# Two transformer blocks on one core: both heads' stick-breaking values in turn, and a projection that begins with three tiles side by side

## The chip, the cores and the metric

The kernel runs on one core of one Trainium2 chip. The metric is the device time of one execution in microseconds; of the runs shown the median is taken. The weights come from memory during the run; nothing of them stays from one execution to the next.

## The reference

Two blocks work on 512 tokens of width 1024. The first has three mixers, whose outputs are gated, added, projected and normed, and a feed-forward part; the second has a gated recurrence, latent attention and two convolutional feed-forward parts. The change touches only the first block's stick-breaking attention (8 heads of 64) and the projection behind the merge:

```python
def stick_breaking_attention(q, k, v):
    # A[t,s] = sigmoid(z_ts) * prod_{s<j<t} (1 - sigmoid(z_tj)), s < t
    def one_block(args):
        q_blk, bi = args
        z = jnp.einsum('bhqd,bhkd->bhqk', q_blk, kf) * scale
        mask = key_pos < qpos
        log1m = jnp.where(mask, jax.nn.log_sigmoid(-z), 0.0)
        excl = lax.cumsum(log1m, axis=3, reverse=True) - log1m
        a = jnp.where(mask, jnp.exp(jax.nn.log_sigmoid(z) + excl), 0.0)
        return jnp.einsum('bhqk,bhkd->bhqd', a, vf)
...
merged = gates[:, :, 0] * y_pool + gates[:, :, 1] * y_sb + gates[:, :, 2] * y_x
h = h + rmsnorm(merged @ w_out[l], norm_mix_post[l])
```

## The kernel before, in words

Activations lie transposed: a tile has 128 features on the partitions and the 512 tokens beside each other; eight tiles are one activation. Every product with a weight is done three times, for precision: high half of the weight by high half of the operand (L225), low by high (L226), high by low (L227). An output tile of 128 features is `pe_tile`: 8 blocks of contraction, 24 products, into one bank of `ps_gemm` (four banks, `m.gb`) or `ps_attend` (four banks, `m.ab`). A unit is the weight of one such tile, 512 KB. There are four slots for units: SyncE loads unit u when GpSimd is done with unit u-4, ScalarE writes its high half (`high`, L200) when TensorE is done with unit u-4, and GpSimd the low half (L2454 and L2455). TensorE waits in `take_unit` for both halves.

The order on each engine is written out by hand, with semaphore waits between them; there is no scheduler. Each of the four stick-breaking rounds (`pe_stick`) does two heads: tiles for query, key and value, the scores of head 0 (L740, and the mask, L743), the values' transposes (L349), two gate tiles, the suffix sums of head 0 (`pe_stick_suffix`, L755), a gate tile, the scores of head 1, head 0's values (`pe_stick_values`, L766), a gate tile, the pooled products, and the suffix sums of head 1. Head 1's values stand behind the query tile of the next round, behind the fourth round behind the first gate tile of the merge. ScalarE makes softplus and its high half from the scores (L827 to L836), VectorE the rest (L906, L909), which is the suffix sums' operand, and ScalarE's exponential (L842) makes the weights that the values multiply. `act_stick_out` (L847) and `dve_stick_low_out` (L892) take both heads' result.

The values are plain fp32 products; in the trace each product has two records and two weight loads. The output has 64 rows: head 0 writes partitions 0 to 63 of bank `ab(3)`, head 1 partitions 64 to 127. The cross attention before it has such products too, L596, in this order (r is the first output partition, 0 for even h and 64 for odd; all 512 tokens wide):

```python
    for j in range(2):
        for h in (2 * j, 2 * j + 1):
            k, r = (h % 2) * 2 + h // 2, 64 * (h % 2)
            for mb in range(2):
                ins = t.op.matmul(m.a_bank[r:r + 64, j * 512:(j + 1) * 512],
```

`pe_merge` does the second gate and the attention's output projection, two tiles at a time; VectorE gates (L996), adds (L1000) and, behind ScalarE's high half (L980), writes the low half of each merged tile (L1002). `pe_project_mix` multiplies the merged tiles by w_out, in eight tiles; ScalarE copies each result out (L1025) and squares it (L281), VectorE adds the squares (L301), and TensorE sums them over the partitions (L257) for the norm. `pe_wide` is the other way to do tiles: three at a time, block of contraction by block, so that it can begin when the first operand is there; the norms' first tiles use it.

Of the kernel before, what the change touches and what calls it, by code (L numbers as in the profile page):

```python
# [7 lines left out]
P = 128  # L8
S = 512
D = 1024  # L10
KD = D // P
# [6 lines left out]
TB = S // P  # L18
TILE = S
# [3 lines left out]
SLOTS = 4  # L23
WIDE = 3
# [5 lines left out]
ZOFF = (0, 512, 1024, 896)  # L30
# [8 lines left out]
ACT = mybir.ActivationFunctionType  # L39
# [67 lines left out]
class Memory:  # L107
# [50 lines left out]
    def bank(self, b, w=512):  # L158
        return self.gb(b, w) if b < 4 else self.ab(b - 4, w)
# [23 lines left out]
def short_unit(m, u):  # L183
    return unit_source(m, u)[0]


def high(m, s):

    if s.ahead:
        s.ahead = False  # L190
        return
    u = s.unit
    s.unit += 1
    if u >= m.n_units:
        return
    j, w = u % SLOTS, UNIT_S if short_unit(m, u) else UNIT
    s.wait_ge(m.s_raw[j], 16 * (u // SLOTS + 1))
    if u >= SLOTS:
        s.wait_ge(m.U.sem, u - SLOTS + 1)
    s.op.activation(m.wh[:, j * UNIT:j * UNIT + w], m.raw[:, j * UNIT:j * UNIT + w], ACT.Copy).then_inc(m.s_hi, 1)  # L200


def unit_of(m, *event):

    return m.U.table[event] - 1


def high_to(m, s, u):

    while s.unit <= min(u, m.n_units - 1):  # L210
        high(m, s)


def take_unit(m, t, ahead=0):

    u = t.unit + ahead
    t.wait_ge(m.s_hi, u + 1)
    t.wait_ge(m.s_lo, u + 1)
    return (u % SLOTS) * UNIT


def products(m, t, out, base, pairs, start=True, stop=True):
    for n, (blk, xh, xl) in enumerate(pairs):
        c = base + blk * P
        t.op.matmul(out, m.wh[:, c:c + P], xh, start=start and n == 0, stop=False, skip_group_check=True)  # L225
        t.op.matmul(out, m.wl[:, c:c + P], xh, start=False, stop=False, skip_group_check=True)  # L226
        ins = t.op.matmul(out, m.wh[:, c:c + P], xl, start=False, stop=stop and n == len(pairs) - 1,  # L227
                          skip_group_check=True)
    return ins


def pe_tile(m, t, event, out, xh, xl, quarters=range(4)):

    base = take_unit(m, t)
    w = TILE
    for q in quarters:
        pairs = [(kb, xh[:, kb * w:(kb + 1) * w], xl[:, kb * w:(kb + 1) * w]) for kb in (2 * q, 2 * q + 1)]
        ins = products(m, t, out, base, pairs, start=q == 0, stop=q == 3)
        if q == 3:
            ins.then_inc(*m.U.mark(*event))  # L240
            t.unit += 1


def pe_wide(m, t, kb, events, xh, xl):

    sl = slice(kb * TILE, (kb + 1) * TILE)
    bases = [take_unit(m, t, n) for n in range(WIDE)]
    for b, base in enumerate(bases):
        ins = products(m, t, m.gb(b), base, [(kb, xh[:, sl], xl[:, sl])], start=kb == 0, stop=kb == KD - 1)
        if kb == KD - 1:  # L250
            ins.then_inc(*m.U.mark(*events[b]))
    if kb == KD - 1:
        t.unit += WIDE


def pe_sum_over_partitions(m, t, event, out, src):
    t.op.matmul(out, m.col("ones", 0, P), src, start=True, stop=True).then_inc(*m.T.mark(*event))  # L257
# [17 lines left out]
def act_square(m, s, stage, j, src, width=TILE):  # L275
    if j == 0:
        s.op.activation(m.ss[:, 0:width], src, ACT.Square).then_inc(*m.A.mark(stage, "square", j))
        return
    if j > 2:
        s.wait_ge(*m.V.at(stage, "sum", j - 2))  # L280
    s.op.activation(m.sq_tile(j % 2, width), src, ACT.Square).then_inc(*m.A.mark(stage, "square", j))  # L281
# [65 lines left out]
def pe_to_tokens(m, t, event, bank, src, blocks):  # L347
    for b in range(blocks):
        ins = t.op.transpose(bank[:, b * P:(b + 1) * P], src[:, b * P:(b + 1) * P], m.col("ident", 0, P))  # L349
    ins.then_inc(*m.T.mark(*event))  # L350
# [353 lines left out]
def stick_tiles(m):  # L704
    c = KD + 4
    lg = [m.big[:, c * TILE + n * ZW:c * TILE + (n + 1) * ZW] for n in range(2)]
    return m.big_tile(KD), m.big_tile(KD + 1), m.big_tile(KD + 2), m.big_tile(KD + 3), lg
# [49 lines left out]
    ins.then_inc(*m.T.mark("stick", "suffix", i, hh))  # L757


def pe_stick_values(m, t, i, hh):  # L760
    _, _, _, vtok, lg = stick_tiles(m)
    r, x = 64 * hh, lg[hh]
    t.wait_ge(*m.A.at("stick", "vtok", i))
    t.wait_ge(*m.A.at("stick", "weights", i, hh))
    for kb in range(TB):
        ins = t.op.matmul(m.a_bank[r:r + 64, 3 * 512 + kb * P:4 * 512], vtok[:, kb * P + r:kb * P + r + 64],  # L766
                          x[:, ZOFF[kb]:ZOFF[kb] + S - kb * P], start=kb == 0, stop=kb == 3, skip_group_check=True)
    ins.then_inc(*m.T.mark("stick", "out", i, hh))


def pe_stick_pooled(m, t, i):
# [14 lines left out]
def stick_bank(m, n, i):  # L786

    return m.gb(n if i else (2, 3, 0)[n])


def pe_stick(m, t, i):
    vt = stick_tiles(m)[2]
    for n, name in enumerate(("q", "k", "v")):
        if i:
            t.wait_ge(*(m.V.at("stick", "pooled", i - 1, 0) if n == 2 else m.V.at("stick", f"gate{2 * n}", i - 1, 1)))
        elif n == 2:
            t.wait_ge(*m.A.at("cross", "kept", 6))
        else:
            continue
        pe_tile(m, t, ("stick", name, i), stick_bank(m, n, i), m.nh, m.nl)  # L800
        if i and n == 0:
            pe_stick_values(m, t, i - 1, 1)
    pe_stick_scores(m, t, i, 0)
    t.wait_ge(*m.V.at("stick", "v", i))
    t.wait_ge(*(m.V.at("stick", "low", i - 1) if i else m.A.at("cross", "kept", 7)))
    pe_to_tokens(m, t, ("stick", "vtok", i), m.ab(3), vt, TB)
    t.wait_ge(*m.V.at("stick", "q", i))
    pe_tile(m, t, ("stick", "gate0", i, 0), m.gb(0), m.nh, m.nl)
    pe_tile(m, t, ("stick", "gate2", i, 0), m.gb(1), m.nh, m.nl)
    pe_stick_suffix(m, t, i, 0)  # L810
    t.wait_ge(*m.V.at("stick", "gate0", i, 0))
    pe_tile(m, t, ("stick", "gate0", i, 1), m.gb(0), m.nh, m.nl)
    pe_stick_scores(m, t, i, 1)
    pe_stick_values(m, t, i, 0)
    t.wait_ge(*m.V.at("stick", "gate2", i, 0))
    pe_tile(m, t, ("stick", "gate2", i, 1), m.gb(1), m.nh, m.nl)
    pe_stick_pooled(m, t, i)
    pe_stick_suffix(m, t, i, 1)
# [132 lines left out]
def pe_merge(m, t):  # L951
    for j in range(0, KD, 2):
        for n in range(2):
            t.wait_ge(*(m.V.at("merge", "gate", j - 2 + n) if j else m.V.at("stick", "gate0" if n == 0 else "gate2", 3, 1)))
            pe_tile(m, t, ("merge", "gate", j + n), m.gb(n), m.nh, m.nl)
            if j == 0 and n == 0:
                pe_stick_values(m, t, 3, 1)
        base = take_unit(m, t)
        t.wait_ge(*m.V.at("stick", "low", 3))
        for n in range(2):  # L960
            t.wait_ge(*(m.V.at("merge", "gated", j - 2 + n) if j else m.V.at("stick", "pooled", 3, n)))
            pairs = [(4 * n + kb, m.bigr[:, O_HIGH + kb * TILE:O_HIGH + (kb + 1) * TILE],
                      m.bigr[:, O_LOW + kb * TILE:O_LOW + (kb + 1) * TILE]) for kb in range(4)]
            products(m, t, m.gb(2 + n), base, pairs).then_inc(*(m.U if n else m.T).mark("merge", "out", j + n))
        t.unit += 1
# [37 lines left out]
                .then_inc(*m.V.mark("merge", "low", j + n))  # L1003


def pe_project_mix(m, t):
    t.wait_ge(*m.V.at("merge", "low", 7))
    for j in range(KD):
        if j < 4:
            t.wait_ge(*(m.V.at("merge", "gate", 6 + j) if j < 2 else m.V.at("merge", "gated", 4 + j)))  # L1010
        else:
            t.wait_ge(*m.A.at("mixed", "kept", j - 4))
        pe_tile(m, t, ("mixed", j), m.gb(j % 4), m.bigr[:, 0:8 * TILE], m.bigr[:, 8 * TILE:16 * TILE])
    t.wait_ge(*m.V.at("mixed", "sum", KD - 1))
    pe_sum_over_partitions(m, t, ("mixed", "total"), m.ab(3), m.ss[:, :])


def act_project_mix(m, s):
    for j in range(KD):
        f = m.big_tile(j)  # L1020
        high(m, s)
        if j == 0:
            s.wait_ge(*m.V.at("merge", "low", 7))
        s.wait_ge(*m.U.at("mixed", j))
        s.op.activation(f, m.gb(j % 4), ACT.Copy).then_inc(*m.A.mark("mixed", "kept", j))  # L1025
        s.wait_ge(*m.A.at("mixed", "kept", j))
        act_square(m, s, "mixed", j, f)
    high_to(m, s, unit_of(m, "ffn0", "up", 0, 0, 0) + WIDE)
    s.tables(LOGEXP)
    s.wait_ge(*m.T.at("mixed", "total"))  # L1030
    act_rstd(m, s, ("mixed", "rstd"), m.rstd2, m.ab(3), D)
# [1643 lines left out]
```

## Time and profile before

| | us |
|---|---|
| median of 3 runs | 2090.29 (2089.08 to 2091.22) |
| the profiled execution itself | 2093.21 |
| its span, first to last instruction | 2091.4 |
| TensorE busy (matmul) | 2038.1 (97%) |
| VectorE, ScalarE, GpSimd busy | 916.7, 909.6, 847.8 |

The span is 1.8 us shorter than the execution that it is part of. PE is TensorE's matmul, PEld its weight load, DVE VectorE, ACT ScalarE, POOL GpSimd. A matmul of 512 columns is shown with some 0.39 us, but the next one starts 0.227 us after it, since they are pipelined: durations of single records overlap, and starts tell the rate. The granted clock is the share of TensorE's full clock of 2.4 GHz that it was given; over the whole span it is 0.992.

### The profile page before, as it was taken

How to read it: one execution, taken by the hardware profiler on the slowest of the kernel's cores; microseconds unless marked ns; L12 is line 12 of the kernel's file. 1: busy time of each engine (PE TensorE's matmuls, PEld its weight loads, DVE VectorE, ACT ScalarE, POOL GpSimd, SP SyncE). 2: the span in 40 equal slices, each digit the busy share in tenths (PEclk: the TensorE clock that was granted, in tenths of full speed). 3: DMA queues.
4: the chain of work that ended last, by engine and by line, in shares of the span. 5: the costliest groups of instructions: out<-in, count | busy, mean ns of one | idle time of the engine just before them, and what ended most of it. 6: DMA issues, size and time to landing. Idle time of an engine off the chain costs nothing.

```text
span 2091.4 us, 23319 instructions
## 1 busy us (share of the span) xinstructions
PE 2038.1 (97%) x9356; PEld 1659.9 (79%) x9356; DVE 916.7 (44%) x1436; ACT 909.6 (43%) x1254; POOL 847.8 (41%) x672
## 2 busy tenths in 40 slices
PE   7999999989999998999999999999999999999999
PEld 6777787768888886788887888888877778888887
DVE  5622223334310323877886355055154544531551
ACT  6455444244323323555555444234256644432441
POOL 1243333435444454233334354444432234444542
PEclk9999999999999999999999999999999999999999
DMA  6122222223333332112121233333310222332332
GB/s 240 51 80 71 81 68 74 81 81 91 101 100 88 104 94 88 41 61 71 52 70 61 81 111 101 101 91 101 100 44 26 84 71 81 111 99 83 106 96 71
DMA packets 51659, 178.09 MB, mean 85 GB/s; under 512 B 5728, under 2 KB 8928, under 8 KB 51424
## 3 DMA queue, kind: packets, MB, share of 16 engines
q1 hardware_dynamic: 51552, 176.61, 27.2%
q8 instruction: 74, 1.21, 0.2%
q14 instruction: 33, 0.27, 0.0%
HBM read 174.49 MB, written 2.10 MB: 84 GB/s over the span
## 4 chain that ended last, share of the span: by engine, by line
PE 93%; DVE 4%; ACT 2%; POOL 1%; issue 1%; DMA 0%; SPq 0%; ACTq 0%
PE ps_gemm L225 24%; PE ps_gemm L227 24%; PE ps_gemm L226 24%; PE ps_attend L225 3%; PE ps_attend L227 3%; PE ps_attend L226 3%; PE ps_attend L1415 2%; PE ps_attend L755 1%; PE ps_attend L2195 1%; PE ps_attend L740 1%; PE ps_attend L766 1%; PE ps_attend L2261 1%; PE ps_attend L2196 1%; PE ps_attend L257 1%; ACT weights_high L200 1%
## 5 line engine op out<-in xcount | busy, mean ns | idle before, releaser
L2454 POOL TENSOR_TENSOR weights_low<-weights_raw,weights_high 128x512 fp32r<-128x512 f32 (+1 forms) x334 | 423.4, 1268 | 1222.1 <-ACT weights_high L200 1221.7
L225 PE MATMUL ps_gemm<-normed_high,weights_high 128*128 128x512 f32 x1672 | 667.4, 399 | 14.5 <-DVE normed_low L286 12.3
L227 PE MATMUL ps_gemm<-normed_low,weights_high 128*128 128x512 f32 x1672 | 653.5, 391 | 0.0
L226 PE MATMUL ps_gemm<-normed_high,weights_low 128*128 128x512 f32 x1672 | 653.3, 391 | 0.0
L200 ACT ACTIVATE weights_high<-weights_raw 128x1024 fp32r<-128x1024 f32 (+1 forms) x341 | 340.7, 1005 | 440.2 <-PE ps_attend L227 208.4
L2455 POOL TENSOR_TENSOR weights_low<-weights_raw,weights_high 128x512 fp32r<-128x512 f32 (+1 forms) x334 | 440.0, 1317 | 0.0
L225 PEld LDWEIGHTS ps_gemm<-normed_high,weights_high 128*128 128x128 f32 x1672 | 315.7, 189 | 86.1 <-DVE normed_low L286 13.9
L226 PEld LDWEIGHTS ps_gemm<-normed_high,weights_low 128*128 128x128 f32 x1672 | 315.8, 189 | 66.6 <-issue 3.8
L227 PEld LDWEIGHTS ps_gemm<-normed_low,weights_high 128*128 128x128 f32 x1672 | 315.2, 188 | 66.8
L225 PE MATMUL ps_gemm<-operands_high_low,weights_high 128*128 128x512 f32 x576 | 227.6, 395 | 6.1 <-DVE operands_high_low L1002 3.3
L227 PE MATMUL ps_gemm<-operands_high_low,weights_high 128*128 128x512 f32 x576 | 225.4, 391 | 0.0
L226 PE MATMUL ps_gemm<-operands_high_low,weights_low 128*128 128x512 f32 x576 | 225.2, 391 | 0.0
L342 DVE TENSOR_TENSOR scratch<-ps_gemm,rstd 128x512 f32<-128x512 f32 x91 | 62.1, 688 | 249.1 <-PE ps_gemm L227 234.2
L342 DVE TENSOR_TENSOR squares<-ps_gemm,rstd 128x512 f32<-128x512 f32 x106 | 73.1, 690 | 173.4 <-PE ps_gemm L227 141.6
L1181 ACT ACTIVATE ps_attend<-squares,parameters 128x512 f32<-128x512 f32 x88 | 68.9, 783 | 170.1 <-DVE squares L342 170.1
L225 PEld LDWEIGHTS ps_gemm<-operands_high_low,weights_high 128*128 128x128 f32 x576 | 108.9, 189 | 30.3 <-DVE operands_high_low L1002 3.7
L225 PE MATMUL ps_attend<-operands_high_low,weights_high 128*128 128x512 f32 (+1 forms) x304 | 117.0, 385 | 10.6 <-DVE operands_high_low L286 10.6
L227 PEld LDWEIGHTS ps_gemm<-operands_high_low,weights_high 128*128 128x128 f32 x576 | 108.7, 189 | 23.1
L226 PEld LDWEIGHTS ps_gemm<-operands_high_low,weights_low 128*128 128x128 f32 x576 | 108.9, 189 | 22.4 <-issue 0.2
L226 PE MATMUL ps_attend<-operands_high_low,weights_low 128*128 128x512 f32 (+1 forms) x304 | 116.2, 382 | 0.0
L227 PE MATMUL ps_attend<-operands_high_low,weights_high 128*128 128x512 f32 (+1 forms) x304 | 116.2, 382 | 0.0
L1235 DVE SCALAR_TENSOR_TENSOR ps_attend<-squares,parameters,ps_attend 128x511 f32<-128x511 f32 x88 | 66.4, 755 | 76.0 <-ACT ps_attend L1181 76.0
(282 smaller groups left out, 2081.7 us busy)
## 6 DMA issues: line engine op xcount, KB each, us to landing
weights_raw<-weights_full SPq DMA_DIRECT2D x317, 512.0 KB, 3.6
weights_raw<-weights_short SPq DMA_DIRECT2D x24, 128.0 KB, 2.1
residual<-x_tiles SPq DMA_DIRECT2D x4, 512.0 KB, 7.5
out_tiles<-residual SPq DMA_DIRECT2D x8, 256.0 KB, 2.1
parameters<-params SPq DMA_DIRECT2D x1, 1559.5 KB, 9.1
scratch<-memory_tiles SPq DMA_DIRECT2D x2, 512.0 KB, 6.9
scratch<-positions SPq DMA_DIRECT2D x1, 256.0 KB, 10.0
parameters<-params SPq DMA_DIRECT2D x1, 136.5 KB, 2.2
```

The lines of the kernel that those rows point to most:

```text
L200: s.op.activation(m.wh[:, j * UNIT:j * UNIT + w], m.raw[:, j * UNIT:j * UNIT + w], ACT.Copy).then_inc(m.s_hi, 1)
L225: t.op.matmul(out, m.wh[:, c:c + P], xh, start=start and n == 0, stop=False, skip_group_check=True)
L226: t.op.matmul(out, m.wl[:, c:c + P], xh, start=False, stop=False, skip_group_check=True)
L227: ins = t.op.matmul(out, m.wh[:, c:c + P], xl, start=False, stop=stop and n == len(pairs) - 1, skip_group_check=True)
L257: t.op.matmul(out, m.col("ones", 0, P), src, start=True, stop=True).then_inc(*m.T.mark(*event))
L342: return v.op.tensor_tensor(dst, ps, m.rstd[:, 0:dst.shape[1]], ALU.mult)
L740: t.op.matmul(zb[:, ZOFF[kb]:ZOFF[kb] + w], k[r:r + 64, kb * P:(kb + 1) * P], q[r:r + 64, kb * P:S], start=kb != 3, stop=False, skip_group ...
L1181: s.op.activation(y, m.sq_tile(half), ACT.Identity, bias=m.col(f"conv_b{n - 1}", c), scale=m.col(f"conv_w{n - 1}", 88 + c)).then_inc(*m.A. ...
L1235: v.op.scalar_tensor_tensor(out=y[:, 1:S], in0=u[:, 0:S - 1], scalar=w(1), in1=y[:, 1:S], op0=ALU.mult, op1=ALU.add).then_inc(*m.V.mark(st ...
L1415: ins = t.op.matmul(m.ab(bank, P, c * P), left[:, c * P:(c + 1) * P], right[:, c * P:(c + 1) * P], start=c == 0, stop=c == TB - 1, skip_gr ...
L2454: g.op.tensor_tensor(m.wl[:, a], m.raw[:, a], m.wh[:, a].bitcast(F32), ALU.subtract)
L2455: g.op.tensor_tensor(m.wl[:, b], m.raw[:, b], m.wh[:, b].bitcast(F32), ALU.subtract).then_inc(m.s_lo, 1)
```

## The change

`pe_stick_values` does both heads, one product of each in turn, and is called once a round, behind the next round's query tile (behind the fourth, behind the merge's first gate tile). It waits for the exponential of head 1. The call for head 0 between head 1's scores and a gate tile is gone. `pe_wide` can take its banks from elsewhere, and the projection's first three tiles go side by side into `ab(0)` to `ab(2)`, each block when its merged tile is there; the other five follow one by one in the `gb` banks. ScalarE converts the unit that a tile frees before it copies that tile out.

```diff
-def pe_wide(m, t, kb, events, xh, xl):
+def pe_wide(m, t, kb, events, xh, xl, bank=None):
+    bank = bank or m.gb
...
-        ins = products(m, t, m.gb(b), base, [(kb, xh[:, sl], xl[:, sl])], start=kb == 0, stop=kb == KD - 1)
+        ins = products(m, t, bank(b), base, [(kb, xh[:, sl], xl[:, sl])], start=kb == 0, stop=kb == KD - 1)
...
-def pe_stick_values(m, t, i, hh):
+def pe_stick_values(m, t, i):
     _, _, _, vtok, lg = stick_tiles(m)
-    r, x = 64 * hh, lg[hh]
     t.wait_ge(*m.A.at("stick", "vtok", i))
-    t.wait_ge(*m.A.at("stick", "weights", i, hh))
+    t.wait_ge(*m.A.at("stick", "weights", i, 1))
     for kb in range(TB):
-        ins = t.op.matmul(m.a_bank[r:r + 64, 3 * 512 + kb * P:4 * 512], vtok[:, kb * P + r:kb * P + r + 64],
-                          x[:, ZOFF[kb]:ZOFF[kb] + S - kb * P], start=kb == 0, stop=kb == 3, skip_group_check=True)
-    ins.then_inc(*m.T.mark("stick", "out", i, hh))
+        for hh in range(2):
+            r, x = 64 * hh, lg[hh]
+            ins = t.op.matmul(m.a_bank[r:r + 64, 3 * 512 + kb * P:4 * 512], vtok[:, kb * P + r:kb * P + r + 64],
+                              x[:, ZOFF[kb]:ZOFF[kb] + S - kb * P], start=kb == 0, stop=kb == 3, skip_group_check=True)
+            if kb == TB - 1:
+                ins.then_inc(*m.T.mark("stick", "out", i, hh))
...
         if i and n == 0:
-            pe_stick_values(m, t, i - 1, 1)
+            pe_stick_values(m, t, i - 1)
...
     pe_stick_scores(m, t, i, 1)
-    pe_stick_values(m, t, i, 0)
     t.wait_ge(*m.V.at("stick", "gate2", i, 0))
...
             if j == 0 and n == 0:
-                pe_stick_values(m, t, 3, 1)
+                pe_stick_values(m, t, 3)
...
+def mixed_bank(m, j):
+    return m.ab(j) if j < WIDE else m.gb(j % 4)
...
 def pe_project_mix(m, t):
-    t.wait_ge(*m.V.at("merge", "low", 7))
-    for j in range(KD):
-        if j < 4:
-            t.wait_ge(*(m.V.at("merge", "gate", 6 + j) if j < 2 else m.V.at("merge", "gated", 4 + j)))
+    hi, lo = m.bigr[:, 0:8 * TILE], m.bigr[:, 8 * TILE:16 * TILE]
+    for kb in range(KD):
+        t.wait_ge(*m.V.at("merge", "low", kb))
+        pe_wide(m, t, kb, [("mixed", j) for j in range(WIDE)], hi, lo, m.ab)
+    for j in range(WIDE, KD):
+        if j < KD - 1:
+            t.wait_ge(*(m.V.at("merge", "gate", 2 + j) if 3 < j < 6 else m.V.at("merge", "gated", 7 if j == 3 else 6)))
         else:
-            t.wait_ge(*m.A.at("mixed", "kept", j - 4))
-        pe_tile(m, t, ("mixed", j), m.gb(j % 4), m.bigr[:, 0:8 * TILE], m.bigr[:, 8 * TILE:16 * TILE])
+            t.wait_ge(*m.A.at("mixed", "kept", 3))
+        pe_tile(m, t, ("mixed", j), mixed_bank(m, j), hi, lo)
...
 def act_project_mix(m, s):
+    first = unit_of(m, "mixed", 0)
+    high_to(m, s, first + WIDE)
     for j in range(KD):
         f = m.big_tile(j)
-        high(m, s)
+        if j < KD - 1:
+            high_to(m, s, first + SLOTS + j)
...
-        s.op.activation(f, m.gb(j % 4), ACT.Copy).then_inc(*m.A.mark("mixed", "kept", j))
+        s.op.activation(f, mixed_bank(m, j), ACT.Copy).then_inc(*m.A.mark("mixed", "kept", j))
```

On TensorE in round 0, before: the mask products of head 1's scores (L743), the values of head 0 (L766) and the gate tile.

```order
L743 MATMUL ps_attend<-operands_high_low 128x128 x4
L766 MATMUL ps_attend<-scratch 64x512
L766 MATMUL ps_attend<-scratch 64x384
L766 MATMUL ps_attend<-scratch 64x256
L766 MATMUL ps_attend<-scratch 64x128
L225 MATMUL ps_gemm<-normed_high,weights_high 128x512
```

At the same place after (lines are 1 to 13 higher there: the mask is L744, the values L769).

```order
L741 MATMUL ps_attend<-scratch 128x384
L741 MATMUL ps_attend<-scratch 128x128
L741 MATMUL ps_attend<-scratch 128x256
L744 MATMUL ps_attend<-operands_high_low 128x128 x4
L225 MATMUL ps_gemm<-normed_high,weights_high 128x512
```

The gate tile follows the scores directly. On TensorE behind the query tile of round 1, after:

```order
L226 MATMUL ps_gemm<-normed_high,weights_low 128x512
L227 MATMUL ps_gemm<-normed_low,weights_high 128x512
L769 MATMUL ps_attend<-scratch 64x512 x2
L769 MATMUL ps_attend<-scratch 64x384 x2
L769 MATMUL ps_attend<-scratch 64x256 x2
L769 MATMUL ps_attend<-scratch 64x128 x2
L225 MATMUL ps_gemm<-normed_high,weights_high 128x512
```

Here stood only the four of head 1; now each width comes twice, once for each head.

## Rows read from the trace of the kernel before

**Rows 1.** The page's part 4, the chain that ended last, by engine

```profile
PE 93%; DVE 4%; ACT 2%; POOL 1%; issue 1%; DMA 0%; SPq 0%; ACTq 0%
```

**Rows 2.** Busy time by stretch (length; busy and instructions by engine)

```profile
100.00:405.00 305.00, 301.71 (x1365) 237.36 (x1365) 88.32 (x102) 142.74 (x146) 118.63 (x89) 1.00 0.25 76
405.00:480.00 75.00, 67.61 (x274) 54.46 (x273) 25.98 (x39) 31.61 (x44) 23.86 (x20) 0.90 0.20 64
```

**Rows 3.** TensorE's waits over the whole span (total us, times, longest)

```profile
PE ps_gemm L225 <- DVE normed_low L286: 12.3, 2, 7.0
...
PE ps_gemm L225 <- DVE operands_high_low L1002: 3.3, 1, 3.3
```

**Rows 4.** The chain in round 2, in order of time (start, us, what)

```profile
255.79 0.59 PE ps_attend L743 x4
256.38 2.30 PE ps_attend L766 x8
258.68 0.43 PE ps_gemm L225
...
269.82 2.72 PE ps_attend L755 x20
272.54 0.28 PE ps_gemm L225
```

**Rows 5.** Instructions of L766 (number, ns min/median/max, starts)

```profile
L766 PEld LDWEIGHTS ps_attend<-scratch x64: 132/137/137, 135.1 to 340.6; 128*64 128x64 f32 x64
L766 PE MATMUL ps_attend<-scratch x64: 272/432/643, 135.1 to 340.7; 128*64 128x512 f32 x16, 128*64 128x384 f32 x16, 128*64 128x256 f32 x16, 128*64 128x128 f32 x16
```

**Rows 6.** L596 alone by stretch (length, then busy time and records in flight)

```profile
86.70:87.20 0.50, 0.50 (x6) 0.17 (x3) 1.00 1.14 270
...
85.80:89.80 4.00, 3.70 (x16) 1.23 (x16) 1.00 0.43 131
```

**Rows 7.** L766 alone by stretch, one block of one head

```profile
135.65:136.15 0.50, 0.50 (x3) 0.21 (x2) 1.00 0.00 0
...
135.10:138.10 3.00, 2.37 (x8) 1.01 (x8) 1.00 0.39 85
```

**Rows 8.** VectorE in order of time, round 2 (start, us, what, idle before)

```profile
263.22 1.49 DVE L909 TENSOR_TENSOR operands_high_low<-scratch,operands_high_low 128x1280 fp32r<-128x1280 f32 x1 [1.34 <-ACT operands_high_low L836]
```

**Rows 9.** ScalarE in order of time, round 2

```profile
266.94 1.28 ACT L103 ACT_TABLE_LOAD   x1
```

**Rows 10.** TensorE in order of time, from the merge to the projection

```profile
400.39 0.39 PE L226 MATMUL ps_gemm<-operands_high_low,weights_low 128*128 128x512 f32 x1
400.62 0.39 PE L227 MATMUL ps_gemm<-operands_high_low,weights_high 128*128 128x512 f32 x1
404.30 0.80 PE L225 MATMUL ps_gemm<-operands_high_low,weights_high 128*128 128x512 f32 x1 [3.29 <-DVE operands_high_low L1002]
...
410.32 0.39 PE L227 MATMUL ps_gemm<-operands_high_low,weights_high 128*128 128x512 f32 x1
```

**Rows 11.** VectorE in order of time, end of the merge

```profile
403.55 0.69 DVE L1002 TENSOR_TENSOR operands_high_low<-scratch,operands_high_low 128x512 fp32r<-128x512 f32 x1 [0.69 <-ACT operands_high_low L980]
```

**Rows 12.** GpSimd in order of time, merge and projection

```profile
399.24 1.74 POOL L2455 TENSOR_TENSOR weights_low<-weights_raw,weights_high 128x512 fp32r<-128x512 f32 x1
...
427.23 1.28 POOL L2455 TENSOR_TENSOR weights_low<-weights_raw,weights_high 128x512 fp32r<-128x512 f32 x1
```

**Rows 13.** ScalarE in order of time, projection

```profile
423.69 0.60 ACT L1025 ACTIVATE scratch<-ps_gemm 128x512 f32<-128x512 f32 x1 [3.23 <-PE ps_gemm L227]
424.32 0.63 ACT L281 ACTIVATE squares<-scratch 128x512 f32<-128x512 f32 x1
424.86 1.05 ACT L200 ACTIVATE weights_high<-weights_raw 128x1024 fp32r<-128x1024 f32 x1
```

**Rows 14.** Busy time and granted clock (PEclk) behind the stall

```profile
404.00:410.00 6.00, 5.70 (x13) 4.46 (x14) 0.24 (x1) 0.47 (x1) 2.51 (x2) 0.50 0.30 89
```

**Rows 15.** The page's part 6, loads of weights (KB each, us to landing)

```profile
weights_raw<-weights_full SPq DMA_DIRECT2D x317, 512.0 KB, 3.6
```
## The prediction

> **What bounds the kernel now.** First the chain that ended last: 93% of the span is TensorE, and the reader is to see that DMA and the queues have nothing in it [rows 1]. So time goes only where TensorE gets less to do, stops waiting, or runs at its higher clock. Then the busy time by stretch [rows 2]: from 100 to 405 us (cross attention, the four stick-breaking rounds, the merge) it is busy 301.7 of 305 us; from 405 to 480 us (projection, norm) 67.6 of 75 us, at a granted clock of 0.90. Then TensorE's waits [rows 3]: the 3.3 us that are missing of the first 305 are one wait, for the last low half of the merge (L1002). The rounds themselves are bound by TensorE's own instructions, and there only a cheaper form of the same products can help. The change addresses one of each: products in the rounds, and the wait at the projection.
>
> **Part 1, the values of both heads in turn.** Today a round has two blocks of values, one per head, each 8 records of 64 output columns (two for each product), 2.30 us on the chain [rows 4]. Behind the first the next gate tile's first product costs 0.43 us on the chain, against 0.28 us behind the suffix products. Taking that block away is worth 2.30 + 0.15 = 2.45 us a round. There are four rounds (64 records, 16 of each width [rows 5]).
> The block behind the next query tile stays and gets both heads, 16 records instead of 8. What those cost is the main question. The heads write different halves of the partitions (0 to 63 and 64 to 127), and this kernel has such a place already: the cross attention's values, L596, with two heads into one bank [rows 6]. It has 16 records of 512 columns in 3.70 us of busy time, 0.23 us for each, while L766 is only half as fast ([rows 7]: 8 records with 2 x 1280 columns in 2.37 us; 2560 columns in 2.37 us is 1080 a us, 8192 in 3.70 us is 2210 a us). In a stretch of half a microsecond six records of L596 are open, of L766 three [rows 6, 7]. So products into the two halves of the columns run beside each other, at full rate each. I expect of the new block what one head's costs, 2.30 us, and a surcharge: the rows show this for 512 columns alone, while the new block goes down to 128 columns, where two loads of 64 columns must fit beside one product. On L743 four products of 128 columns, each with a load of 128 columns, follow each other in 0.59 us, 0.15 us each [rows 4]; two loads of half that width should need about the same, against 0.11 us that a record of 128 columns takes of L766's rate (128/1080). That concerns two of the eight pairs, so 0.1 us a round, with an end of the second product that lies a little behind the first's. Bounds: 0 us, and, if no second load were hidden, 8 x 0.137 = 1.1 us a round [rows 5].
> Part 1: 4 x (2.45 - 0.1) = 9.4 us.
> The Trainium skill (TensorE: Matmul & The Clock Gate, "Part 3: Packing small matmuls") says that products in different column groups run concurrently, but that a weight load overlaps with products in flight only where the row group differs, and that products start in strict order. Both heads use all 128 rows here, so by that rule the second load of each pair is bare, and the sum would be 4.4 us smaller. The trace disagrees: on L596 the order in the program is four records of one head, then four of the other, and six are open at once with no loss of rate for the loads [rows 6]. I go by the trace, and keep the rule as a rival.
>
> **What the missing block covered.** It stood between the scores of head 1 and the second gate tile, while ScalarE and VectorE work from these scores to the suffix products' operand. In round 2 this operand (L909) is done at 263.22 + 1.49 = 264.71 us [rows 8], and the suffix products stand at 269.82 us [rows 4]. They move to 267.4 us: 2.7 us of cover are left. The exponential behind them (L842) finds ScalarE free: its table load ends at 268.22 us [rows 9], and the suffix ends at 267.4 + 2.7 = 270.1 us. Nothing new is late. The weight units too: a tile takes 5.4 us, their ScalarE and GpSimd work 1.04 + 2 x 1.29 = 3.6 us [rows 12, 13]. The wait of the joined block is the one that head 1's block has now, with the same query tile as cover. Head 0's result comes later, but its first user is the next round's softplus (L827), which waits for scores that stand behind the value block in TensorE's own order.
>
> **Part 2, three tiles side by side.** Before, the first tile waits for all eight merged operands: the last product before it starts at 400.62 us, would hand over at 400.85, and the next starts at 404.30 us [rows 10]: 3.45 us. That stall has a second price: the granted clock is 0.50 (of 2.4 GHz, so 1.2) from 404 to 410 us [rows 14], and the 14 products that start from 404.30 to 410.01 us take until 410.32, 6.02 us [rows 10]; 14 x 0.227 (the spacing of the rows from 400.39 to 400.62 and on) is 3.18. So 2.84 us more.
> After, the first 54 products (six operands, three tiles, three products each) need only what is long done; the seventh and eighth operand are asked for at 401 + 54 x 0.227 = 413.3 us, and are there at 404.24 [rows 11]. What is late next is a weight unit: the three tiles need three units at the start. The third's low half is done by GpSimd at 399.24 + 1.74 = 400.98 us [rows 12]; with 0.06 us for the hand-over (as from L1002's end, 404.24, to 404.30) TensorE starts at 401.05 instead of 400.85: 0.2 us, which I count as no matter for the clock, a fifteenth of the stall that brought it down. Bounds 0 and 0.7 us.
> Behind the wide part: it ends at 401.05 + 72 x 0.227 = 417.4 us and frees three units at once. The fourth tile's unit is converted by then: ScalarE takes it ahead of its first copy, as today. The fifth tile's is needed at 417.4 + 5.44 = 422.8 us, and ScalarE's turn (1.04) comes first in its queue now, then GpSimd (2.6 to 3.0): 421.1 to 421.5. That is 1.3 us of slack. The next comes behind a copy and a square (0.60 + 0.63 [rows 13]) and has 4 us. On ScalarE copy and square of each tile lie 1.04 us further back, except for the last tile, which has no conversion ahead of it: the tail from the last product to the norm (squares' sum, its total on TensorE) stays as it is. The same 192 products run in either form, and the banks that the wide tiles use (the scores' three) were last read by the exponential of the last round, ahead of the values.
> Part 2: 3.45 + 2.84 - 0.2 = 6.1 us.
>
> **Later stages.** Their instructions are the same. Two later stalls (12.3 us together, the longer 7.0 [rows 3]) are of the same kind, and behind the first the clock falls too: 6 us at 0.50 alone would leave 0.96 in the stretch from 405 to 480 us, and it has 0.90 [rows 2]. How long that lasts need not be the same when everything comes 15 us earlier. I take 0, with 1.5 us either way.
>
> **Sum.** 9.4 + 6.1 = 15.5 us. The profiled execution took 2093.21 us (span 2091.4 and 1.8 around it), 2.9 us over the median 2090.29 of the runs shown; 2093.21 - 15.5 = 2077.7, on the scale of the median 2074.8. I take 2075.
>
> **Rivals.**
> A: the columns' halves don't run beside each other in this block, or loads are bare. With none, the new block costs 4.6 us and only the 0.15 of an entry is saved each round: total 6.1 + 0.6, 2083.6 us. With bare loads 2079.2 us. For it: widths below 512 are not in the rows. Against it: L596 [rows 6].
> B: part 2 gives back half: the fifth tile's unit misses its 1.3 us, or three units at the start come 1 us late and the clock falls all the same: 2078 us. For it: GpSimd's second half took 1.74 us where VectorE was at work, 1.29 elsewhere [rows 12].
> C, slower: the wide part holds three of four unit slots for 16.4 us, and the pipeline behind runs empty. If each of the four narrow tiles then had to wait for a whole load, ScalarE and GpSimd (3.6 + 1.04 + 2.6 = 7.2 us [rows 12, 13, 15]) against 5.44 us of products, 1.8 us are lost four times, 7 us, and at 1.2 GHz a tile costs 24 x 0.2 = 4.8 us more, 19 us in four: 26 us, against 15.5 gained, 2101 us. It decides once the chain is over 5.44 us. Against it: the load of a unit waits only for GpSimd's work on the slot's old one, so it is in place long before.
> D: the later stretches at 0.50 change by 3 us in all: 2072 or 2078.
>
> **How the numbers follow.** Forecast 0.74 (own range 2073 to 2077.5); A 0.10; B 0.07; D 0.06, half each way; C 0.02; nothing of it works, 0.01. Range 2072 to 2080: the rest of A and C lies above it. 0.2% is 4.2 us, about what a measurement of this kernel tells from none. Faster by more than that holds for all but C and the last: 0.96; same 0.02; slower 0.02.
>
> **What would show it.** Right: the values' line has 64 records as before, in four blocks of 16 and 2.3 to 2.5 us, with five to six open in half a microsecond; none between the scores and the second gate tile; the suffix products follow without a wait; no wait for L1002's successor, at most 0.3 us for L2455 at the projection, and a granted clock of 1.00 from 395 us on to the projection's end, its last product 15 us earlier than 450.47. Wrong: value blocks of 4.6 us, a wait before the suffix products, or TensorE waiting for weights_low behind the wide part.

## The result, and the profile after

The changed kernel takes 2076.57 us (median of 4 runs, 2076.51 to 2076.94) against 2090.76 us before (4 runs): ratio 0.993, 95% interval 0.9919 to 0.9942, which is 12.1 to 16.9 us less; the medians are 14.2 us apart. Measured again beside two variants (below) it was 2075.83 against 2090.57 us, ratio 0.9931 (0.9919 to 0.9944). Forecast were 2075 us, and 2072 to 2080. All ratios here are of executions in the fast state, so that of part 1 alone leaves out one of its five executions (2287.48 us, at a granted clock of 0.846). The profiled execution took 2076.51 us with a span of 2074.7; the one of before 2093.21 and 2091.4.

The chain that ended last is TensorE for 93% of the span, as before. From the scores of round 1's head 1 to the values in round 3, to be read beside [rows 4] (line numbers are a few higher, the values are L769):

```profile
191.23 0.59 PE ps_attend L744 x4
...
249.37 0.59 PE ps_attend L744 x4
...
260.93 2.72 PE ps_attend L756 x20
263.65 0.28 PE ps_gemm L225
...
269.17 2.30 PE ps_attend L769 x16
```

From one round's head 1 scores to the next's it is 58.14 us (249.37 - 191.23). In the chain of before, the second of these places is at 255.79 us [rows 4], and the first is:

```profile
195.21 0.59 PE ps_attend L743 x4
```

That is 60.58 us, so a round is 2.44 us shorter. The gate tile now follows the scores directly; its first product takes 0.28 us on the chain. The suffix products (L756) follow their neighbours with no wait between. The joined block shows 16 records in the 2.30 us that 8 took.

First all value products of after, then the block of round 0 alone by stretch: the length, the busy time, and in brackets the records that touch the stretch, which are called in flight below. Weight loads follow in the same form, then the granted clock.

```profile
L769 PE MATMUL ps_attend<-scratch x64: 272/432/643, 152.8 to 329.3; 128*64 128x512 f32 x16, 128*64 128x384 f32 x16, 128*64 128x256 f32 x16, 128*64 128x128 f32 x16
```

```profile
152.80:155.30 2.50, 2.37 (x16) 1.06 (x16) 1.00 0.74 203
153.30:153.80 0.50, 0.50 (x6) 0.21 (x4) 1.00 0.82 131
```

The number of records is that of before, and so is the duration of one (least 272, median 432 ns, as in [rows 5]). But twice as many run in the 2.37 us of [rows 7], and six are in flight in half a microsecond instead of three. The widths below 512 cost nothing extra either: at all four widths a record of head 1 starts 0.006 us behind its neighbour of head 0, and the last two pairs, 128 columns wide, start 0.11 us apart (154.809 and 154.919 us), as L766's last two records do.

The operand of the suffix products (L912) is done at 256.81 + 1.49 = 258.30 us, 2.6 us ahead of them:

```profile
256.81 1.49 DVE L912 TENSOR_TENSOR operands_high_low<-scratch,operands_high_low 128x1280 fp32r<-128x1280 f32 x1 [1.34 <-ACT operands_high_low L839]
```

TensorE from the merge to the projection, beside [rows 10]:

```profile
389.29 0.39 PE L227 MATMUL ps_gemm<-operands_high_low,weights_high 128*128 128x512 f32 x1
389.80 0.47 PE L225 MATMUL ps_attend<-operands_high_low,weights_high 128*128 128x512 f32 x1
...
433.19 0.39 PE L227 MATMUL ps_gemm<-operands_high_low,weights_high 128*128 128x512 f32 x1
```

From the merge's last product to the projection's first it is 0.51 us from start to start where it was 3.68 us; the usual distance is 0.23, so 0.28 us are lost. GpSimd's second half of the third unit ends at 387.92 + 1.74 = 389.66 us, 0.14 us before the first product, so the third tile's weight is what came last:

```profile
387.92 1.74 POOL L2468 TENSOR_TENSOR weights_low<-weights_raw,weights_high 128x512 fp32r<-128x512 f32 x1
```

The clock stays at 1.00, here in the first 6 us (the granted clock stands behind the last engine's busy time) and in fact to the projection's last product, against 0.50 in [rows 14]:

```profile
389.80:395.80 6.00, 6.00 (x27) 4.97 (x28) 2.39 (x4) 1.58 (x2) 2.54 (x2) 1.00 0.29 87
```

Behind the three tiles side by side, the fifth tile's unit is converted by ScalarE and GpSimd from 405.11 to 408.80 us. The fourth tile's products run until 411.65, so the unit is there 2.85 us early, and the fifth tile starts at the usual distance of 0.23 us.

```profile
405.11 1.06 ACT L200 ACTIVATE weights_high<-weights_raw 128x1024 fp32r<-128x1024 f32 x1 [11.97 <-PE ps_attend L227]
```

### The profile page after: what moved, and what is told of

The parts are those of the page before. It is cut to its first block, busy times and chain, and to the rows that moved or that the text cites. A ratio compares the mean times of both kernels' runs of the same rounds, so it can differ in the third digit from the quotient of the medians.

```text
span 2074.7 us, 23325 instructions
## 1 busy us (share of the span) xinstructions
PE 2026.1 (98%) x9356; PEld 1653.8 (80%) x9356; DVE 919.0 (44%) x1436; ACT 909.0 (44%) x1254; POOL 848.9 (41%) x672
## 4 chain that ended last, share of the span: by engine, by line
PE 93%; DVE 3%; ACT 2%; POOL 1%; issue 1%; DMA 0%; SPq 0%; ACTq 0%
PE ps_gemm L225 24%; PE ps_gemm L227 23%; PE ps_gemm L226 23%; PE ps_attend L225 3%; PE ps_attend L227 3%; PE ps_attend L226 3%; PE ps_attend L1428 2%; PE ps_attend L756 1%; PE ps_attend L2208 1%; PE ps_attend L741 1%; PE ps_attend L2274 1%; PE ps_attend L2209 1%; PE ps_attend L258 1%; PE ps_gemm L1414 0%; PE ps_attend L1457 0%
## 5 line engine op out<-in xcount | busy, mean ns | idle before, releaser
L225 PE MATMUL ps_gemm<-normed_high,weights_high 128*128 128x512 f32 x1672 | 666.4, 399 | 14.2 <-DVE normed_low L287 12.0
L225 PEld LDWEIGHTS ps_gemm<-normed_high,weights_high 128*128 128x128 f32 x1672 | 315.3, 189 | 85.9 <-DVE normed_low L287 14.4
L225 PE MATMUL ps_gemm<-operands_high_low,weights_high 128*128 128x512 f32 x552 | 217.5, 394 | 2.8 <-POOL weights_low L2468 2.4
L227 PE MATMUL ps_gemm<-operands_high_low,weights_high 128*128 128x512 f32 x552 | 215.7, 391 | 0.0
L226 PE MATMUL ps_gemm<-operands_high_low,weights_low 128*128 128x512 f32 x552 | 215.6, 391 | 0.0
L225 PE MATMUL ps_attend<-operands_high_low,weights_high 128*128 128x512 f32 (+1 forms) x328 | 126.2, 385 | 9.5 <-DVE operands_high_low L287 9.4
L227 PE MATMUL ps_attend<-operands_high_low,weights_high 128*128 128x512 f32 (+1 forms) x328 | 125.4, 382 | 0.0
L226 PE MATMUL ps_attend<-operands_high_low,weights_low 128*128 128x512 f32 (+1 forms) x328 | 125.4, 382 | 0.0
L225 PEld LDWEIGHTS ps_gemm<-operands_high_low,weights_high 128*128 128x128 f32 x552 | 104.1, 189 | 25.7 <-issue 3.0
L227 PEld LDWEIGHTS ps_gemm<-operands_high_low,weights_high 128*128 128x128 f32 x552 | 104.1, 189 | 21.8
L226 PEld LDWEIGHTS ps_gemm<-operands_high_low,weights_low 128*128 128x128 f32 x552 | 104.0, 188 | 21.4 <-issue 0.2
```

## The experiments

Gains in us are taken from the ratios (1 minus the ratio, of before's median), unless medians are named; "over the change" compares with the change's 0.993. Beside them stretches of the traces are compared: at an undisturbed clock they repeat to 0.01 us, while whole executions of one kernel differ by two and more. **Rounds** is from a product of round 0's second scores (number 571 of the 9356 records) to the last product of the merge, **projection** from there to the projection's last product. Before: 266.59 and 49.85 us. After: 256.79 and 43.89, in both profiles of it.

### The parts alone

One kernel is the change with `pe_project_mix` and `act_project_mix` as they were; of the edit, its heart:

```diff
-    for kb in range(KD):
-        t.wait_ge(*m.V.at("merge", "low", kb))
-        pe_wide(m, t, kb, [("mixed", j) for j in range(WIDE)], hi, lo, m.ab)
-    for j in range(WIDE, KD):
...
+    t.wait_ge(*m.V.at("merge", "low", 7))
+    for j in range(KD):
...
```

> Part 1 alone: both heads' values in one block behind the query tile, the projection as before. Theory (halves of the columns run beside each other, the cover at the suffix products lasts): a round takes 2.44 us less, four 9.8 us, so 2090.5 - 9.8 = 2080.7 us, and the stall of 3.3 us and the half-speed stretch at the projection are still there. Rival (part 1 gives less and part 2 more than they seem to in one trace): 2083 us or more.

Measured: 2081.63 against 2091.95 us, ratio 0.9953 (0.9939 to 0.9966), 9.8 us by the ratio (the medians are 10.3 apart). Rounds 256.79, as after. The stall is there again, but this time without a fall of the clock: the 6 us behind it are at 1.00.

```profile
PE ps_gemm L225 <- DVE operands_high_low L1005: 3.3, 1, 3.3
```

```profile
395.00:401.00 6.00, 6.00 (x27) 4.94 (x28) 0.00 (x0) 0.31 (x2) 2.55 (x2) 1.00 0.28 87
```

The other kernel is the one before with these two functions and `pe_wide` of the change; again the heart of it:

```diff
+    for kb in range(KD):
+        t.wait_ge(*m.V.at("merge", "low", kb))
+        pe_wide(m, t, kb, [("mixed", j) for j in range(WIDE)], hi, lo, m.ab)
...
```

> Part 2 alone: the projection begins with three tiles side by side, the values stay in two blocks a round. Theory: the stall (3.45 us) goes, 0.3 us of waiting for a weight unit comes, and the clock stretch goes with the stall; in the one profile of before that stretch cost 2.8 us, but the medians of the whole change are 1.3 us nearer to each other than the two profiles, so that a typical execution loses less to it: 4.5 to 6.0 us in all, 2084.5 to 2086 us. Rival (all of the sum of one profile holds in every run): 2084.4 us. Rival (the wide form gives most back): 2088 us.

Measured: 2086.08 against 2091.95 us, ratio 0.9975 (0.9966 to 0.9984), 5.2 us by the ratio (the medians are 5.9 apart). Rounds 266.59 as before, projection 43.88. The parts add up: 9.8 and 5.2 us are 15.0, and the whole is 14.4 to 14.6 by its two ratios.

### The order of the heads in the block

Here the four products of head 0 stand first, then the four of head 1:

```diff
-    for kb in range(TB):
-        for hh in range(2):
+    for hh in range(2):
+        for kb in range(TB):
```

> The whole change, but in the joined block the four products of head 0 stand before the four of head 1. Theory (each half of the columns has its own queue, and products of one half pass those of the other, as on L596): the block still takes 2.3 us, and the time is that of the change, 2076.6 us. Rival (products start in strict order, so only the seam overlaps and the order in turn is what matters): block 4.2 us, 4 x 1.9 = 7.6 us more, 2084 us.

Measured: 2082.26 against 2091.95 us, ratio 0.9957 (0.9945 to 0.997), 5.6 us over the change. Rounds 262.93, 6.14 more. Neither theory had it right: the block is between the two. By stretch, the block of round 0:

```profile
151.00:157.50 6.50, 3.93 (x16) 1.81 (x16) 1.00 0.29 81
...
152.80:153.30 0.50, 0.50 (x3) 0.16 (x2) 1.00 0.49 197
153.40:153.80 0.40, 0.40 (x5) 0.30 (x5) 1.00 0.96 389
154.20:154.70 0.50, 0.50 (x3) 0.26 (x2) 1.00 0.10 41
```

It takes 3.93 us. It has three records in flight at first, five in its middle (in 0.40 us), and three again. The widths tell the heads apart: head 1's first record, 512 columns wide, starts at 153.339 us, 0.006 us behind the fifth of head 0 (256 wide, 153.333) and ahead of head 0's last three (153.549, 153.764, 153.874). So it passes three records still to come, but not seven: head 1 can overtake, and only over a short distance. So neither the theory of a queue for each half holds, nor that of starts in strict order.

Now two products of a head, then two of the other:

```diff
-    for kb in range(TB):
-        for hh in range(2):
+    for kb, hh in ((0, 0), (1, 0), (0, 1), (1, 1), (2, 0), (3, 0), (2, 1), (3, 1)):
+        if True:
```

> The whole change, but in the joined block two products of head 0 stand before two of head 1, and again. With the four of a head in a row (e3) the block took 3.9 us, and head 1's first record started with the fifth of head 0, four records (two products) ahead of its turn; on L596, with groups of two products, the heads overlapped fully. Theory (a record can start beside another when at most some four records of the other half stand ahead of it): groups of two are within that reach, the block takes 2.3 to 2.5 us and the time is that of the change, at most 0.8 us over it. Rival (a run of products of one head always holds the other's back in part): block 2.9 us or more, 2.4 us or more over the change.

Measured: 2077.86 us (2075.68 to 2078.54) against 2090.57, ratio 0.9936 (0.9923 to 0.9948); the change in the same comparison has 2075.83 (2075.14 to 2079.18). The medians are 2.0 us apart, more than the 0.8 expected at most, but the ranges overlap and don't tell the two kernels apart. The trace does: rounds 256.91, 0.12 us over the change for all four rounds, block 2.42 us.

```profile
151.00:157.50 6.50, 2.42 (x16) 1.23 (x16) 1.00 0.25 81
```

Head 1's first record starts 0.014 us behind head 0's first, ahead of three that stand before it in the program: again three are passed. This is the order of L596 [rows 6]. The order in turn is the safe one, not the only one.

### Both heads in the same half of the columns

```diff
-            ins = t.op.matmul(m.a_bank[r:r + 64, 3 * 512 + kb * P:4 * 512], vtok[:, kb * P + r:kb * P + r + 64],
-                              x[:, ZOFF[kb]:ZOFF[kb] + S - kb * P], start=kb == 0, stop=kb == 3, skip_group_check=True)
+            ins = t.op.matmul(m.a_bank[0:64, 3 * 512 + kb * P:4 * 512], vtok[:, kb * P + r:kb * P + r + 64],
+                              x[:, ZOFF[kb]:ZOFF[kb] + S - kb * P], start=kb == 0 and hh == 0, stop=kb == 3 and hh == 1, skip_group_check=True)
```

> The whole change, but both heads of the joined block are written to partitions 0 to 63 of the bank, so that they share one half of the columns; the attention's result is another one (the two heads are added there, and the other half is left as it was). Same products, same order, same waits. Theory (the gain is that the two halves run beside each other): the block takes 4.5 us instead of 2.3, and the time rises by 4 x 2.2 = 8.8 us to 2085.4. Rival (the gain comes from the joined block having one seam with the neighbours less, or from loads that are better hidden): under 2 us more, 2078.5 at most.

Measured: 2084.29 against 2091.95 us, ratio 0.9965 (0.9953 to 0.9977), 7 us over the change; rounds 265.28, 8.49 more.

```profile
151.00:157.50 6.50, 4.52 (x16) 2.06 (x16) 1.00 0.26 81
153.30:153.80 0.50, 0.50 (x3) 0.19 (x2) 1.00 0.62 213
```

This kernel adds the two heads up in one half, so its attention is another one, and only its time counts. With the same products, order and waits the block takes 4.52 us, 2.15 more, and three records are in flight. So, by the traces, 8.5 of the 9.8 us of part 1 come from the two halves working beside each other. What is left, 266.59 - 265.28 = 1.3 us in four rounds, comes with there being one block a round where there were two, each with a start and an end of its own.

### What in part 2 brings the gain

The three tiles side by side are kept here, but the wait for all eight operands is back:

```diff
     for kb in range(KD):
-        t.wait_ge(*m.V.at("merge", "low", kb))
+        t.wait_ge(*m.V.at("merge", "low", 7))
```

> The whole change, but the three tiles side by side wait for all eight merged operands first, as the projection did before. Theory (the gain of part 2 is the wait alone, and the clock behind it): the stall of 3.3 to 3.5 us is back before the projection, with a granted clock of 0.50 behind it, and the time is that of part 1 alone, 4.5 to 6 us over the change, 2081 to 2082.6. Rival (the form with three tiles itself brings something): under 3 us over the change.

Measured: 2081.22 against 2091.57 us, ratio 0.9951 (0.9939 to 0.9964). Projection 49.67 us, as before; the stall is back (3.3 us, for L1005), and the clock is at 0.54 in the 6 us behind it. Three tiles side by side without the finer waits bring nothing; the projection is 0.2 us shorter than before's, and the clock is at 0.54 where that has 0.50 (more on this below).

```profile
392.00:398.00 6.00, 6.00 (x15) 4.76 (x16) 0.00 (x0) 0.13 (x1) 2.51 (x2) 0.54 0.24 87
```

The other way round, the tiles follow one by one, with a finer wait in the first (the edit is against part 1 alone):

```diff
-    t.wait_ge(*m.V.at("merge", "low", 7))
+    t.wait_ge(*m.V.at("merge", "low", 5))
...
+        if j == 0:
+            pe_tile(m, t, ("mixed", j), m.gb(j), hi, lo, (0, 1, 2))
+            t.wait_ge(*m.V.at("merge", "low", 7))
+            pe_tile(m, t, ("mixed", j), m.gb(j), hi, lo, (3,))
...
```

> Part 1, and for the projection the form of before, eight tiles one by one, but the first tile waits for six merged operands only and for the last two ahead of its last quarter. Six operands are 18 products, 4.1 us, and the last operand came 3.4 us after the last product of the merge, so no wait should be left; and only one weight unit is needed at the start, not three. Theory (all that counts is that the last two operands are covered): as the change or 0.3 us better, 2076.2 to 2076.6, with no wait at the projection. Rival (the three tiles are needed for cover, the seventh or eighth operand comes too late for one tile): a wait of 0.5 us or more, and 2077.5 us or over.

It was measured a second time, on one chip with the change itself:

> Part 1 and the projection tile by tile, with the wait for the last two merged operands ahead of the first tile's last quarter, once more and beside the change itself. Theory (it saves the 0.28 us of the third tile's weight unit and nothing else): 0.3 us under the change. Rival (its lead in the first comparison, 0.7 us, is real): 0.7 us or more under. Rival (no difference): the same.

> The change itself once more, to be compared with the two beside it on one chip. Expected 2076.6 us, with 0.28 us lost at the projection's start to the weight unit of the third tile.

Measured: first 2075.83 against 2091.57 us, ratio 0.9926 (0.9913 to 0.994). The second time it took 2076.49 (2075.96 to 2077.71) against the change's 2075.83 (2075.14 to 2079.18), so the medians don't tell them apart. In both traces its projection is 43.52 us against 43.89. Of these 0.37 us, 0.28 are the wait for the third tile's weight: here the first tile follows the merge at the usual distance. The other 0.09 lie among the products.

```profile
388.76 0.39 PE L227 MATMUL ps_gemm<-operands_high_low,weights_high 128*128 128x512 f32 x1
388.99 0.39 PE L225 MATMUL ps_gemm<-operands_high_low,weights_high 128*128 128x512 f32 x1
```

So the three tiles side by side aren't needed: the products of one tile for its first six operands are 4.1 us, and the last operand came 3.4 us after the hand-over from the merge in before [rows 10, 11]. The finer wait is the gain. The 0.37 us are too small for the medians.

### What the stall costs

Two kernels were profiled once more, each in a single execution:

> Part 1 alone once more, for a second profile. In its first profile the stall of 3.45 us at the projection was there, but the products behind it ran at full clock, while three other profiles with that stall (before, before again, all waits kept) show 6.8 us at 0.50. Theory (whether the clock falls behind a stall of this length differs from execution to execution, so the price of the stall is 3.45 us for certain and 2.8 more in some): either is possible here; the two profiles of this kernel differ or agree, but the stall is again 3.45 us. Rival (with part 1 the clock never falls there): full clock again.

> The kernel before once more, for a second profile of it. Its first profile was 2.9 us over its median. Theory (what differed was the start, and how long the clock stays at 0.50 behind the stall at the projection): this profile shows about 2090.5 us with the same rows in rounds and merge, and a half-speed stretch of another length than 6.8 us behind the stall. Rival: the same stretch again, and the difference lies elsewhere.

Measured: part 1 alone again 2081.13 us, before again 2091.92 us. The 6 us behind the stall are, in part 1 alone again and then in before again:

```profile
393.40:399.40 6.00, 6.00 (x19) 4.78 (x20) 0.00 (x0) 0.12 (x1) 2.53 (x2) 0.72 0.25 87
```

```profile
403.00:409.00 6.00, 5.91 (x14) 4.65 (x15) 0.03 (x1) 0.26 (x1) 2.51 (x2) 0.51 0.31 87
```

The second profile of before has the same stretch of low clock as the first (projection 49.79 us), against the expectation. What differs is its start: the product where rounds are counted from is at 132.8 us instead of 134.0. Such a shift isn't the change's doing either: in the two profiles of part 1 alone that product is at 134.4 and 132.9 us.

Part 1 alone lost less to the clock the second time than before does, but more than the first time, so the rival (never, with part 1) is out. The five profiles with the stall have 49.85, 49.79, 49.67, 48.75 and 47.13 us for the projection. The stall itself is 3.45 us in each. With the stall and at full clock it would be 47.06 (3.68 from start to start, and the 43.38 of after's 192 products). What is over that is 2.8, 2.7, 2.6, 1.7 and 0.1 us, 2.0 in the mean; the 0.1 was at full clock and is no loss to it.

The size follows from how much of the low stretch the products fall into. In before the clock is at 0.50 from 403.4 to 410.2 us, of which 5.9 us lie behind the restart at 404.30. In part 1 alone again it falls only 1.4 us behind the restart at 393.36, and is back 3.4 us later:

```profile
394.80:398.10 3.30, 3.30 (x9) 2.54 (x9) 0.00 (x0) 0.00 (x0) 1.33 (x2) 0.50 0.26 76
```

At half the clock, half of such a time is lost: 2.9 and 1.7 us, against the 2.8 and 1.7 above.

## Why the prediction was right, point by point

- **Part 1's main question, what the joined block costs:** right. The rows of L596 carried over to the narrow widths, and the rule by which the second load would be bare does not hold here: with 16 loads the block takes what it took with 8. The term "4 x (2.45 - 0.1) = 9.4" was 9.8, since the 0.1 us surcharge is not there. It rested on a wrong reading of L743: the 0.59 us on the chain, divided by four, hold the start and the end of the block too. The starts of its four products (134.557, 134.720, 134.832 and 134.945 us) are 0.11 us apart but for the first, although each has a load of 128 columns. That is the rate of L766's and the joined block's last products, and would have given no surcharge.
- **The cover of the missing block:** right. 2.6 us are left at the suffix products, 2.7 were forecast, and nothing waits in the rounds.
- **Part 2's wait:** right. The stall of 3.45 us went, and the third tile's weight unit costs 0.28 us where 0.2 was forecast. The form that was credited with it, three tiles side by side, isn't what does it; the finer wait is.
- **Part 2's clock:** right for the profile it was read from, and risky as a term for a median. The 2.84 us come from one execution; over five with the same stall it is 2.0 in the mean, though both profiles of before itself have 2.7 and 2.8. With 2.0 the sum would be 9.8 + 3.45 + 2.0 - 0.28 = 15.0. The medians are 14.2 and 14.7 us apart, with an interval of 12.1 to 16.9, so they don't tell 15.5 from 15.0: that the clock is why less was measured is not shown. Part 1 too low by 0.4 and the clock too high by up to 0.8 cancel in part, and that part of the hit is luck.
- **Behind the wide part:** right, no wait. The slack was 2.85 us where 1.3 was reckoned: the three units don't come free at once. The first tile's last product stands before the others', and its unit's conversion starts at 405.11 us, 1.1 us before the wide part ends.
- **Later stages, taken as 0 with 1.5 us either way:** from the projection's last product to the last product of the kernel it is 1637.34 us before and 1637.92 after, well within that. Behind a wait for a weight unit that both have (1.8 us after, 1.9 before) the clock falls in the profile after:

```profile
1686.00:1692.00 6.00, 4.66 (x14) 3.69 (x15) 5.80 (x6) 4.25 (x8) 5.94 (x4) 0.72 0.34 96
```

In that of before it stays at 1.00 there. This is the execution and not the change: of the two profiles of part 1 alone one has the fall and 1637.89 us, the other has none and 1637.29. Rival D, 3 us either way, is out for these profiles.

- **The two profiled executions** differ by 16.7 us, more than the sum of 15.5: 1.5 us of it lies ahead of the rounds, where the changed kernel's work is the same, and differs as much between the two profiles of part 1 alone. With rounds, projection and the rest, 1.5 + 9.8 + 6.0 - 0.6 = 16.7. So the projection's last product came 17.3 us earlier, not 15.

Rival A (halves that don't run beside each other, or bare loads) is out: with both heads in one half the block takes 4.52 us, in the change 2.37, with its 16 loads in it. B and C (units late behind the wide part, the pipeline running empty) are out: from 380 us to the projection's last product the view of waits lists none for TensorE, and the clock is 1.00; the 0.28 us at its start are too short for it.

What stays open: why behind the same stall of 3.45 us the clock falls early in one execution, late in another and not at all in a third. The runs show that it does, and what each costs, not what decides it. Of a record's reach, they show three records passed in both orders, not whether records, products or loads are what is counted.

## What to carry to other kernels

Products of 64 output rows that go to different halves of the partitions should stand next to each other in the program, in turn or at most two and two: they then cost half. In this kernel one head's block alone takes the 2.37 us that both heads take together. When a surcharge is read from a chain, take the starts of the single products: a block's time divided by their number holds its start and end too. And a stage that waits for all its operands before the first product needs a finer wait before it needs another form: count what the first tile can do with the operands that are there, and cover the last ones with it. Of a stall, count the idle time for certain, and the clock behind it only from several profiles: here it was anything from nothing to 2.8 us.

## What the runs showed of the hardware that was not expected

- How far a product may overtake: with four products (8 records) of the other half ahead, it started with the fifth record, not the first (block 3.93 us); with two (4 records) ahead, 0.014 us behind the first (2.42 us). In both cases it passed three records that had not started.
- Where the products stand strictly in turn, the two halves start 0.006 us apart for all four widths, and the pair takes no longer than one alone.
- A stall of the same length, 3.45 us, leaves the granted clock at 1.00, 0.72 or 0.50 to 0.54 over the 6 us behind it, and the first two are executions of one kernel.
